# A fused two-layer transformer kernel: the second quarter of the conditioning product moved into the attention's steps, and a router with fewer VectorE operations

## What is computed

```python
# first block
y = concatenate([rms_norm(y_attention), rms_norm(y_lru), rms_norm(y_conv)])
x = x + y @ w_out
h2 = rms_norm(x, norm2_g)
logits_c, logits_f = h2 @ router_coarse, h2 @ router_fine       # 4 groups, 4 x 8 experts
grp = argmax(logits_c); top2 = top_k(logits_f[grp], 2)
gate = softmax(top2) * softmax(logits_c)[grp]
x = x + sum over the two experts e of a token: gate * ((silu(h2 @ w_gate[e]) * (h2 @ w_up[e])) @ w_down[e])
# second block: two layers, each modulated by a condition vector
shift, scale, gate = split(silu(cond) @ ada_w[l] + ada_b[l], 3)  # cond: c and c_ctx; ada_w is [2, 1024, 3072]
```

## Time and profile before

| | us |
|---|---|
| median of three runs | 2303.55 (2301.32 to 2305.32) |
| the profiled execution, its own time | 2303.85 |
| span of its trace | 2302.0 |
| TensorE busy | 2155.8 (94% of the span) |
| VectorE busy | 1363.5 (59%) |
| ScalarE busy | 1030.9 (45%) |
| GpSimd busy | 365.7 (16%) |

### The profile page before, as it was taken

One profiled execution on the slowest core, in us unless ns is written; L12 is line 12 of the kernel. 1 busy time (PEld: TensorE's weight loads), 2 busy tenths in 40 slices (PEclk: granted clock), 3 DMA queues, 4 the chain that ended last, 5 costly groups with the idle time before them and its releaser, 6 DMA issues.

```text
span 2302.0 us, 26467 instructions
## 1 busy us (share of the span) xinstructions
PE 2155.8 (94%) x10531; PEld 1547.5 (67%) x10531; DVE 1363.5 (59%) x1805; ACT 1030.9 (45%) x1516; POOL 365.7 (16%) x263
## 2 busy tenths in 40 slices
PE   7999999898799998998879999988999999999998
PEld 6877755674576575575568777744555577788886
DVE  5787277466876466465482265567666566533385
ACT  4265466521676466465453244346544523402231
POOL 2000012000210010010100000012665623000014
PEclk9999999999899999999989999999999999999999
DMA  4111030117999999999662101130010031211141
GB/s 130 60 51 37 28 129 29 73 58 293 412 407 422 419 410 394 406 404 399 250 223 64 50 10 33 42 117 1 1 37 19 26 121 74 76 55 37 38 164 64
DMA packets 105888, 348.77 MB, mean 152 GB/s; under 512 B 21960, under 2 KB 54737, under 8 KB 79776
## 3 DMA queue, kind: packets, MB, share of 16 engines
q1 hardware_dynamic: 95040, 321.70, 36.4%
q0 software_dynamic: 9504, 21.08, 2.4%
q10 hardware_dynamic: 1216, 4.24, 0.5%
HBM read 323.21 MB, written 34.26 MB: 155 GB/s over the span
## 4 chain that ended last, share of the span: by engine, by line
PE 76%; DMA 9%; DVE 8%; ACT 5%; issue 2%; SPq 0%; POOL 0%; DVEq 0%; ACTq 0%; POOLq 0%
PE psm L236 72%; DMA mem<-in_exp_w_up_dram 4%; DMA mem<-in_ada_w_dram 2%; DMA mem<-in_exp_w_gate_dram 2%; PE psm L1173 1%; ACT mem L1255 1%; DMA mem<-in_exp_w_down_dram 1%; PE psm L2040 1%; PE psm L527 1%; DVE r L350 1%; DMA mem<-in_odd_w_out_dram 1%; ACT mem L1209 1%; DVE r L394 1%; ACT r L385 1%; DVE mem L3226 0%
## 5 line engine op out<-in xcount | busy, mean ns | idle before, releaser
L236 PE MATMUL psm<-r,r 128*128 128x512 f32 (+6 forms) x6513 | 1546.6, 394 | 67.0 <-DVE r L2206 13.8
L236 PEld LDWEIGHTS psm<-r,r 128*128 128x128 f32 (+3 forms) x6513 | 1198.7, 190 | 399.2 <-issue 79.9
L236 PE MATMUL psm<-mem 128*64 128x512 f32 (+11 forms) x2870 | 466.5, 449 | 21.8 <-DMA mem<-in_ada_w_dram 10.5
L394 DVE TENSOR_TENSOR r<-mem,r 128x1024 fp32r<-128x1024 f32 x240 | 283.3, 1224 | 162.1 <-ACT r L385 159.3
L236 PEld LDWEIGHTS psm<-mem 128*64 128x64 f32 (+5 forms) x2870 | 206.3, 152 | 220.7 <-issue 164.0
L385 ACT ACTIVATE r<-mem 128x1024 fp32r<-128x1024 f32 x240 | 240.0, 1054 | 100.7 <-DMA mem<-in_exp_w_gate_dram 43.4
L3745 POOL TENSOR_TENSOR mem<-mem 128x1024 f32<-128x1024 f32 x63 | 153.3, 2433 | 147.8 <-ACT mem L3697 75.4
L3697 ACT ACTIVATE mem<-psm 128x512 f32<-128x512 f32 x160 | 94.4, 596 | 125.4 <-PE psm L236 118.6
L350 DVE TENSOR_TENSOR r<-mem,r 128x1024 fp32r<-128x1024 f32 (+2 forms) x72 | 76.9, 1111 | 79.3 <-ACT r L341 79.0
L3522 DVE TENSOR_REDUCE small<-psm 128x1 f32<-128x1024 f32 x64 | 78.2, 1221 | 66.5 <-PE psm L236 66.4
L1303 DVE TENSOR_TENSOR_SCAN mem<-mem,small 128x128 f32<-128x128 f32 (+7 forms) x64 | 83.7, 1356 | 24.3 <-POOL mem L1319 20.2
(11 more groups left out here) (375 smaller groups left out, 1754.9 us busy)
## 6 DMA issues: line engine op xcount, KB each, us to landing
mem<-in_exp_w_gate_dram SPq DMA_DIRECT2D x64, 1024.0 KB
mem<-in_exp_w_up_dram SPq DMA_DIRECT2D x64, 1024.0 KB
mem<-in_exp_w_down_dram SPq DMA_DIRECT2D x64, 1024.0 KB
mem<-in_ada_w_dram SPq DMA_DIRECT2D x32, 768.0 KB, 4.2
mem<-in_odd_w_in_dram SPq DMA_DIRECT2D x10, 1024.0 KB
mem<-in_x_dram SPq DMA_DIRECT2D x16, 512.0 KB, 6.6
mem<-in_w_in_dram SPq DMA_DIRECT2D x8, 1024.0 KB
mem<-y2d SPq DMA_DIRECT2D x8, 1024.0 KB, 7.0
```

Of the source, the lines that this page charges most:

```text
L236: return p.e.matmul(o, l, r, start=start, stop=stop, skip_group_check=True)
L394: p.e.tensor_tensor(l, mem(self.raw(i), [R * n])[:, w * q:w * q + w], h.bitcast(F32), SUB).then_inc(*self.lo_done.up(i, q))
```

## The change

Quarter 1 of the conditioning is treated as quarter 0 was: sixteen pieces at steps 1, 2, 4, 6, 8, 10, 11, 13, 15, 17, 19, 20, 22, 24, 26 and 28. Eight units (quarters 2 and 3) instead of twelve are left behind the output product; TensorE takes units 0 to 4 before the router's matmuls and 5 to 7 after them. The places that the pieces of the experts wait for follow this. In the router, several pairs of VectorE operations become one, the running sums over token blocks become matmuls on TensorE, eight comparisons become two operations, and the table is written in whole numbers directly.

```diff
-            for u in range(5, 8):
+            for u in range(5, 16):
                 early_fetch(p, u)
...
-                elif s - 2 in EARLY_STEP and EARLY_STEP[s - 2] == 7:
-                    ada_rows(p, 0)
+                elif s - 2 in EARLY_STEP and EARLY_STEP[s - 2] % 8 == 7:
+                    ada_rows(p, EARLY_STEP[s - 2] // 8)
...
         def out_squares_scalar(p, half, t):
-            p.wait_ge(*ada_pe.at("early", 7))
+            p.wait_ge(*ada_pe.at("early", 15))
...
         def out_rsqrt(p, half, t):
-            p.wait_ge(*ada_out.at(3))
+            p.wait_ge(*ada_rest_out.at(7))
...
-        EARLY_STEP = {3 * u + 3: u for u in range(8)}
+        EARLY_STEP = {1 + 27 * u // 15: u for u in range(16)}
...
-            for i in range(12):
+            for i in range(8):
                 ada_fetch(p, i)
...
         def onehot(p, o, i, v, n, iota, idx, *key):
             p.then(p.e.tensor_tensor(o, i, bcast(v, n), ALU.is_equal), rt_dve, "eq", *key)
-            p.then(p.e.tensor_scalar(o, o, -64.0, 64.0, MUL, ADD), rt_dve, "far", *key)
-            p.then(p.e.tensor_tensor(o, o, iota, ADD), rt_dve, "at", *key)
+            p.then(p.e.scalar_tensor_tensor(o, o, -64.0, iota, MUL, ADD), rt_dve, "at", *key)
...
-            for i in range(1, 8):
-                p.then(e.tensor_tensor(PR[:, i, :], PR[:, i - 1, :].bitcast(F32), OO[:, i - 1, :].bitcast(F32), ADD), rt_dve, "pr", i)
-            e.tensor_tensor(TOT, PR[:, 7, :].bitcast(F32), OO[:, 7, :].bitcast(F32), ADD).then_inc(*rt_dve.up("tot"))
-            p.wait_ge(*rt_pe.at("tot"))
+            p.wait_ge(*rt_pe.at("pos"))
...
-            p.then(e.tensor_scalar(NV, CN, 0.0, None, ALU.is_gt), rt_dve, "nv", 0)
-            for k in range(1, 8):
-                p.then(e.scalar_tensor_tensor(NV, CN, float(128 * k), NV, ALU.is_gt, ADD), rt_dve, "nv", k)
+            p.then(e.tensor_scalar(NV, CN, 1.0 / 128, 12582912.0, MUL, ADD), rt_dve, "further blocks")
+            p.then(e.tensor_scalar(NV, NV, 12582912.0, 0.0, SUB, MAX), rt_dve, "nv")
...
         def router_tensor(p):
-            mm(p, ps[:, 0:256], EVERY, PR.rearrange("p a b -> p (a b)"), False, True).then_inc(*rt_pe.up("pos"))
-            mm(p, ps[:, 0:32], EVERY, TOT, True, True).then_inc(*rt_pe.up("tot"))
+            for i in range(7):
+                mm(p, ps[:, 32 * i + 32:256].rearrange("p (a b) -> p a b", b=32), EVERY,
+                   OO[:, i, :].unsqueeze(1).broadcast_to([128, 7 - i, 32]), False, i == 6)
+            for i in range(8):
+                last = mm(p, ps[:, 256:288], EVERY, OO[:, i, :], i == 0, i == 7)
+            last.then_inc(*rt_pe.up("pos"))
...
         def table_vector(p):
-            p.then(p.e.scalar_tensor_tensor(ROW, ps, -1.0, ROW, ADD, ADD), rt_dve, "row")
-            whole(p, TOK, ROW, 2, "token")
-            p.e.tensor_copy(TAB, TOK).then_inc(*rt_dve.up("tab"))
-            p.e.tensor_copy(TROW, ROW).then_inc(*rt_dve.up("rows"))
+            p.then(p.e.scalar_tensor_tensor(TROW, ps, -1.0, ROW, ADD, ADD), rt_dve, "rows")
+            p.e.tensor_scalar(TAB, TROW, 1, None, ALU.logical_shift_right).then_inc(*rt_dve.up("tab"))
...
-            first = {0: [n2_pe.at("logits", 1)], 1: [ada_pe.at(9)], 2: [n2_pe.at("logits", 1)], 3: [ada_pe.at(7)], 4: [ada_pe.at(8)],
+            first = {0: [n2_pe.at("logits", 1)], 1: [ada_pe.at(4)], 2: [n2_pe.at("logits", 1)], 3: [ada_pe.at(7)], 4: [ada_pe.at(3)],
...
             norm2_tensor(p)
             router_tensor(p)
-            ada_tensor(p, 5, 10)
+            ada_tensor(p, 5, 8)
             table_tensor(p)
-            ada_tensor(p, 10, 12)
             experts_tensor(p)
```

More of the change, by code:

```diff
@@ L1535, in ada_fetch @@
         def ada_fetch(p, i):
-            g, k = 1 + i // 4, i % 4
+            g, k = 2 + i // 4, i % 4
             if i in ADA_AFTER:
@@ L1757, in onehot @@
             p.then(p.e.tensor_tensor(o, i, bcast(v, n), ALU.is_equal), rt_dve, "eq", *key)
-            p.then(p.e.tensor_scalar(o, o, -64.0, 64.0, MUL, ADD), rt_dve, "far", *key)
-            p.then(p.e.tensor_tensor(o, o, iota, ADD), rt_dve, "at", *key)
+            p.then(p.e.scalar_tensor_tensor(o, o, -64.0, iota, MUL, ADD), rt_dve, "at", *key)
             p.then(p.e.tensor_reduce(idx, o, AX, MIN), rt_dve, "first", *key)
-            p.then(p.e.tensor_tensor(o, iota, bcast(idx, n), ALU.is_equal), rt_dve, "hot", *key)
+            p.then(p.e.tensor_tensor(o, o, bcast(idx, n), ALU.is_equal), rt_dve, "hot", *key)
         def whole(p, o, i, n, *key):
@@ L1873, in table_vector @@
             p.then(p.e.tensor_scalar(ROW, ps, 0.0, 8192.0, ALU.is_equal, MUL), rt_dve, "none")
[L1874 to L1878 removed]
+            p.then(p.e.scalar_tensor_tensor(TROW, ps, -1.0, ROW, ADD, ADD), rt_dve, "rows")
+            PB.frees(("tab",), rt_dve.at("rows"))
+            p.e.tensor_scalar(TAB, TROW, 1, None, ALU.logical_shift_right).then_inc(*rt_dve.up("tab"))
             order_vector(p)
@@ L1887, in router_scalar @@
             p.e.activation(e2, e2, ACT.Exp).then_inc(*rt_act.up("e2"))
-            for g in range(1, 3):
-                ada_rows(p, g)
+            ada_rows(p, 2)
         def router_tensor(p):
```

62 lines of the change are left out of this document (29 added, 33 removed).

## The result

| | before | after |
|---|---|---|
| median of the runs | 2303.92 us (11 runs, 2300.08 to 2309.35) | 2308.14 us (11 runs, 2305.03 to 2313.52) |
| ratio to before, 95% interval | | 1.002 (1.0012 to 1.0028) |
| span of the profiled execution | 2302.0 us | 2306.3 us |
| attention: its 44 opening matmuls to the first `x36` group of its end | 281.07 to 422.55, 141.5 us | 281.94 to 436.42, 154.5 us |
| output product done (first logits matmul, `128*36`) | 535.71 | 548.75 |

The change costs 4.2 us; 4.75 us of gain were forecast. (The 2303.55 above is of three runs of the kernel before, the 2303.92 of eleven.) The end of the experts is the wait of 4.4 us that both traces show behind the last block (1134.88 before, 1140.16 after). The table has the error: the attention pays 13.0 us where 5.7 were forecast, the experts' stage gains 7.8 where 10.8 were.

The account below looks back on a forecast made before the run. TensorE was taken to bound the experts' first 100 us, the weight queue afterwards. 2303.85 + 5.7 (attention) - 10.8 (experts' stage) = 2298.75 us, 4.75 us under the median of 2303.55; range 2294.0 to 2305.5.

Parts of the forecast that it names:

- Part 1: Attention: eight more pieces and one more bias, 6.6 us less 0.9 absorbed, cost 5.7 us, between 4.0 and 6.6.
- Part 4: Experts' weight queue: landings come 11.9 us earlier from piece 26 on; stage gains 10.8 us, between 5.2 and 15.3.
- that cover: Attention, step 15: second bias and piece keep TensorE busy during `ada_rows(0)`; costs nothing, or 1.3 us if not.
- Rival C: Start of the experts: TensorE's lower clock eats the earlier start, stage gains 1.0 us, sum 2308.6; chance 0.12.
- 0.9 us "absorbed": Attention: TensorE's existing waits take up 0.9 us of the added 6.6, between 0 and 2.6.
- Part 2: Queue after the output product: four units, 6.29 MB, leave the busy stretch, worth at most 15.3 us at 411 GB/s.
- Part 3: Start of the experts: router chain and gather finish sooner, first product at 593.5, 5.2 us earlier.
- the dry stretch: Weight queue near the experts' start: it runs empty for 1.8 us before piece 10 lands at 603.3.
- the first six waits: Experts: TensorE's idle waits up to 874.69, 12.6 us in all, would vanish; 6.7 us of that needed.
- Rival B: Experts' stage: TensorE paces it for longer, gaining only its start and two or three waits, 6 us, sum 2303.6; chance 0.16.
- Rivals A: Experts' stage: the queue never runs dry, so the stage gains 13.5 to 15.3 us, sum 2295.2; chance 0.15.
- What would show it: Trace signs: attention's last step 5 to 6 us later, experts' first product 5 us earlier, no TensorE wait before about 780.

Follow-up runs that it names:

- e5: The changed kernel with its sixteen pieces at other steps, so none is due before silu is ready and quarter 0's copy falls in step 18; 2305.09 us.
- e4: The changed kernel with its pieces at other steps, the first at step 3 and quarter 1's from step 16; 2307.72 us.
- e7: The changed kernel with quarter 1's pieces multiplied but not fetched, reading quarter 0's weights; 2311.53 us.
- e8: The changed kernel with one of two slices of each unit behind the attention fetched and multiplied twice, 6.29 MB fewer; 2304.68 us.
- e2: The kernel before with only the new router, no quarter moved; 2303.48 us, ratio 0.9995.
- e10: The kernel of e2 with the router's matmuls behind unit 3 of the conditioning instead of unit 4; 2303.82 us.
- e6: The kernel of e5 with the router's matmuls behind unit 3 of the conditioning instead of unit 4; 2300.54 us, ratio 0.9986 to before.
- e11: The kernel of e6 unchanged, run again for a second profile; 2301.39 us, ratio 0.9983 to before.
- e1: The changed kernel with the router of before, so only the quarter is moved; 2308.93 us, ratio 1.0018 to before.
- e9: The kernel of e6 with pieces 8 to 15 cut to 768 columns, the other 768 as two more units behind the attention; 2302.23 us.
- e12: The kernel of e9 with those 768 columns spread over all four groups of output rows, 192 each; 2300.38 us, ratio 0.9985 to before.

## Why the prediction was wrong

The attention cost 7.3 us more than forecast and the stage gained 3.0 less, so Part 1 holds the larger part of the miss and Part 4 the smaller.

- **Part 1, the attention, failed on two steps.** The matmuls were sized right (6.6; 7.0 in e5 with everything in it). "`ada_rows(0)` moves to step 15 ... Nothing, if that cover holds; 1.3 us if not": the cover did not hold, because the second bias needs the very bank that `ada_rows(0)` empties; in e4, where it doesn't come at once, the copies of the next step are late instead. And the first bias was taken as a cost of 0.85 wherever it stands, though in step 1 its silu isn't ready. The two waits are 2.0 us together; the range of 4.0 to 6.6 held neither, though the text had named 1.3 for one. What nothing in it held is that TensorE falls to 1.2 GHz behind each: 3.4 us by the clock, 4.3 together with the waits by e5, since other waits get shorter. 1.7 us more are the third fall, a matter of luck. Rival C had looked for the lower clock only at the start of the experts.
- The sentence on the waits of the attention read one row as all: 0.65 us stands there twice in most rounds, beside waits of 0.25, 1.46 and 1.90 us.
- The 0.9 us "absorbed" were not: e5 pays 7.0 for 6.6. The `w_out` loads ahead of the fetch of step 4 cost nothing (e7).
- **Part 2, the bytes**, 15.3 us at 411 GB/s: right as a ceiling, and no more than that. In e8 the same number of bytes again shows nothing in the trace's stage and 3.5 us in the runs.
- **Part 3, the start**, was sized at 5.2 us and came to 4.3. The sixteen matmuls took 1.96 us where 2.23 were taken. `TAB` was ready 0.4 us late against the forecast, because TensorE reached the router's matmuls 0.5 us late; the gather took 8.87 us for 8.46, and the rest is in the turns. That the table took 3.58 us at the lower clock instead of 1.96 cost nothing: it ended at 593.60, and VectorE came free for it at 593.54. Piece 0 landed at 587.33, 574.3 on the clock of before, against 573.5 by the same bytes: right.
- **Part 4, what the queue makes of it, failed.** Piece 10 was issued at 612.06, or 599.0 on the clock of before, against the forecast 598.4: right, and the dry stretch came. The step that failed is "of it 4.9 must stay. The landings therefore come 5.2 + 11.6 - 4.9 = 11.9 us earlier from there on, and TensorE follows by losing the first six waits". Where 4.9 us were to stay, piece 26 took 7.5, and came 8.7 us earlier than Part 4 has it before, not 11.9. Piece 46 landed 11.4 us after its issue, 7.0 us earlier than before, and one wait was lost, not six. The waits from the experts' 185th us on stand in every kernel, 29 to 32 us with the last one, whatever the queue had moved before.
- **Rival B** ("TensorE paces the stage for longer ... TensorE gets only its start and two or three waits: stage 6") is nearest to what happened: start 4.3 and one wait of 1.9. All waits together are 1.6 us less, and the other 1.9 of the 7.8 stand where TensorE shows no wait. By the table, first product to the end of the experts took 535.8 to 536.2 us with nothing moved (before, e2, e10) and 532.6 to 535.1 with the quarter moved, so beyond the start the bytes gained between 0.7 and 3.6 us. By rival B the sum would be 2303.6; with the attention as it was, 7.3 more.
- **Rivals A and C** did not come: the queue ran dry, and the stage gained 7.8 us, neither 14.4 nor 1.0. That C's sum, 2308.6, is next to the measured 2308.14 is luck.
- **The sum**: its terms make 5.1 us of gain. The forecast of 4.75 sets a sum for the profiled execution against a median 0.3 us lower, and by its own numbers that is 4.80.
- **What would show it**: the dry stretch came, the attention's end was 14 us late instead of 5 to 6, and "the first wait among the experts where it is now, or its waits still 20 us or more" came true in its second half, which was the sign of the wrong step. The "wait for `ada_w` in step 4" and the "sixteen router matmuls over 3 us" did not come. "No TensorE wait before about 780" came true (the first is at 792.43, 779.4 on the clock of before), but it was a weak sign: for it only the wait at 726.98 had to go.

What stays open: e6's and e11's runs gain 2.3 and 0.8 us more over e5 than their start explains, e4's runs gain less than its attention promises, and why the clock falls behind one wait and not behind another of the same length. Single executions, of which each trace is one, differ by more than that in parts that no edit touched.

## What to carry to other kernels

A queue that is full in every slice doesn't make its bytes worth their time: ask who paces the issues behind the place where bytes are taken away, and how long the lead lasts. Work slipped between the steps of a full engine is priced by its matmuls only if it finds its operands, its bank and its helper's copy ready; a wait of about 1 us there was followed, seven times in eight, by 1.7 us or more lost in clock. And when two things are late one after the other, here the landing of the first weights and the router, judge their edits together and try them apart.

## What the runs showed of the hardware

- A DMA share of 0.99 to 1.01 went with 365, 381, 389, 408 and 421 GB/s in different stretches. It tells that transfers are outstanding, not that the rate is reached.
- Waits of 0.65 us, which come back in every round of the attention, left the clock at 1.00. Behind the wait of 0.97 us before the first bias it fell to the lower level in all four traces that have it (after, e1, e7, e8), behind the 1.07 us before the second in three of them (not in e7), behind the 1.90 us near the attention's end in eight of fourteen, and behind the 1.96 us of e4 not. e6 and e11 are one kernel and differ in this. A fall cost 1.7 us, at the first bias of e1 and e7 3.4.
- Four matmuls on four groups of 32 output rows took 0.85 us together, two of them 0.83 (e9, e11), and four of half the columns 0.53 (e12).
